# Conditioning vectors stationary, weights streamed in four column groups: the adaLN products of a two-layer flow block

## The reference, cut to what matters

```python
def ada_params(cond, w, b):            # w: (1024, 6144) per layer
    m = jax.nn.silu(cond) @ w + b
    return [t[:, None, :] for t in jnp.split(m, 6, axis=-1)]

sh1, sc1, g1, sh2, sc2, g2 = ada_params(c, ada_w[i], ada_b[i])
csh1, csc1, cg1, csh2, csc2, cg2 = ada_params(c_ctx[None, :], ada_w[i], ada_b[i])
a = modulate(rmsnorm(h), sh1, sc1)     # h * (1 + scale) + shift
h = h + g1 * rmsnorm(mixer(a))
h = h + g2 * rmsnorm(ffn(modulate(rmsnorm(h), sh2, sc2)))
```

## Time and profile before

| | |
|---|---|
| runs | 2705.26, 2714.47, 2714.45 us; median 2714.45 |
| profiled execution | span 2699.9 us from the first to the last instruction; the median lies 14.6 us above it |
| PE busy | 2432.5 us, 90% of the span |
| DVE, ACT busy | 1322.1 us (49%), 1144.3 us (42%) |
| chain that ended last | PE 79%, DVE 9%, ACT 6%, issue 4% |
| HBM read | 470 MB, 175 GB/s over the span |

### The profile page before, as it was taken

The page is one execution under the profiler, slowest core; times in us unless marked ns, Lnnn a source line. Parts: engine busy times, 40 slices in busy tenths (PEclk is TensorE's granted clock), DMA queues, the critical chain, the costliest instruction groups (busy, mean ns, idle before and its releaser), DMA issues.

```text
span 2699.9 us, 29721 instructions
## 1 busy us (share of the span) xinstructions
PE 2432.5 (90%) x10632; PEld 1840.9 (68%) x10633; DVE 1322.1 (49%) x1694; ACT 1144.3 (42%) x1436; POOL 36.1 (1%) x32
## 2 busy tenths in 40 slices
PE   4899977969999999688968999999999999999997
PEld 1455655538888888354657878787877777878785
DVE  1111045031111123315727878787964446878786
ACT  1201114141111112414435767676753335767675
POOL 0000013000000000000000000000000000000000
PEclk9998988878898889898979999999999999999999
DMA  6232300213333332210015979797964445979783
GB/s 225 94 125 94 125 0 1 82 43 121 120 132 124 125 125 94 90 63 1 12 54 207 359 281 363 269 366 272 362 229 156 164 163 189 359 280 357 295 344 138
DMA packets 68226, 472.56 MB, mean 175 GB/s; under 512 B 8119, under 2 KB 10328, under 8 KB 11544
## 3 DMA queue, kind: packets, MB, share of 16 engines
q1 hardware_dynamic: 64560, 463.50, 46.2%
q10 hardware_dynamic: 3560, 7.76, 0.8%
HBM read 470.18 MB, written 1.05 MB: 175 GB/s over the span
## 4 chain that ended last, share of the span: by engine, by line
PE 79%; DVE 9%; ACT 6%; issue 4%; ACTq 1%; DMA 1%; POOL 1%; DVEq 0%; POOLq 0%
PE bank L366 49%; PE bank L437 7%; PE bank L359 3%; PE bank L575 2%; PE bank L869 2%; DVE w_lo L1641 2%; PE bank L608 2%; ACT w_hi L1161 2%; PE bank L376 1%; PE bank L651 1%; PE bank L408 1%; PE bank L771 1%; PE bank L751 1%; PE bank L845 1%; DVE hT L1304 1%
## 5 line engine op out<-in xcount | busy, mean ns | idle before, releaser
L1641 DVE TENSOR_TENSOR w_lo<-ring,w_hi 128x1024 fp32r<-128x1024 f32 x672 | 797.4, 1222 | 208.1 <-ACT w_hi L1161 182.7
L1161 ACT ACTIVATE w_hi<-ring 128x1024 fp32r<-128x1024 f32 x672 | 697.7, 1059 | 266.0 <-PE bank L366 266.0
L366 PE MATMUL bank<-w_hi,x_hi 128*128 128x512 f32 x1008 | 409.6, 406 | 44.8 <-DVE x_lo L1682 24.3
L366 PE MATMUL bank<-w_hi,x_lo 128*128 128x512 f32 x1008 | 399.0, 396 | 0.0
L366 PE MATMUL bank<-w_lo,x_hi 128*128 128x512 f32 x1008 | 398.5, 395 | 0.0
L366 PEld LDWEIGHTS bank<-w_hi,x_hi 128*128 128x128 f32 x1008 | 193.3, 192 | 100.6 <-issue 43.3
L366 PEld LDWEIGHTS bank<-w_hi,x_lo 128*128 128x128 f32 x1008 | 192.8, 191 | 42.6
L366 PEld LDWEIGHTS bank<-w_lo,x_hi 128*128 128x128 f32 x1008 | 193.7, 192 | 38.4
L366 PE MATMUL bank<-w_hi,h_hi 128*128 128x512 f32 x504 | 196.9, 391 | 13.0 <-DVE h_lo L1655 13.0
L366 PE MATMUL bank<-w_hi,h_lo 128*128 128x512 f32 x504 | 196.7, 390 | 0.0
L366 PE MATMUL bank<-w_lo,h_hi 128*128 128x512 f32 x504 | 196.1, 389 | 0.0
(11 more groups left out here) (283 smaller groups left out, 2957.1 us busy)
## 6 DMA issues: line engine op xcount, KB each, us to landing
ring<-in_moe SPq DMA_DIRECT2D x336, 1024.0 KB, 5.5
ring<-in_pre SPq DMA_DIRECT2D x105, 1024.0 KB, 4.8
hT<-in_xT ACTq DMA_DIRECT2D x1, 2048.0 KB
out_T<-hT SPq DMA_DIRECT2D x2, 512.0 KB, 2.9
arena<-in_q_up ACTq DMA_DIRECT2D x1, 768.0 KB, 5.3
arena<-in_w_krv ACTq DMA_DIRECT2D x1, 640.0 KB, 3.8
mT<-in_decay ACTq DMA_DIRECT2D x1, 512.0 KB
arena<-in_dft ACTq DMA_DIRECT2D x1, 512.0 KB
```

The source lines that it names most:

```text
L366: m = pe.matmul(out, x[a], w[b], start=(first and n == 0), stop=(last and n == 2))
L1161: act.activation(w_hi[:, h % 4, :], ring[:, s % SLOTS, (h % 2) * UNIT:(h % 2 + 1) * UNIT], ACT.Copy).then_inc(sem("w_high"), 1)
L1641: dve.tensor_tensor(w_lo[:, h % 4, :], ring[:, (N_PRE + n) % SLOTS, (h % 2) * UNIT:(h % 2 + 1) * UNIT], w_hi[:, h % 4, :].bitcast(F32), AL ...
```

## The change

1. All 48 ada slots are now done with the conditioning vectors stationary. `cond32` holds the two vectors in a 32-column block with zeros behind them. A slot holds four of the eight 128-feature blocks of the contraction for 512 outputs. The four matmuls of a slot (`ada_half`) write partitions 0 to 31, 32 to 63, 64 to 95 and 96 to 127 of one bank, 512 columns each; the second slot of a group adds onto it. So a group is two slots and 512 outputs, and there are 12 groups per layer (`ADA_G`).
2. ACT copies the 128x512 bank to SBUF, and four matmuls with 2 columns (`ada_columns`) sum the four partial results and turn them, with `pick`, a 128x2 sum of four unit columns, as moving operand.
3. The groups lie elsewhere: 4 ahead of the input projection (as many slots as before), 8 in the SSD loop, one per two rows, 1 behind the first norm sum after the output projection, 11 in the dense SwiGLU, one per two steps. Nothing is interleaved with the input and output projections any more.
4. The gate/up split parts have two buffers (`gw_hi`, `gw_lo`; the second lies in `aT`), and ACT and DVE prepare step q+1 while PE does step q.

```diff
@@ PE @@
-            def ada_slot(s, dst, j, rounds=0):
-                slot_wait(s, rounds)
-                for h in range(2):
-                    for k in range(KD):
-                        m = pe.matmul(dst[:, 2 * (j + h):2 * (j + h) + 2], slot_tile(s, h, k), cond[:, k, :],
-                                      start=(k == 0), stop=(k == KD - 1))
+            def ada_half(g, half, dst):
+                for j in range(4):
+                    m = pe.matmul(dst[32 * j:32 * j + 32, :], cond32[:, 4 * half + j, :],
+                                  ring[:, (ada_slot(g) + half) % SLOTS, j * 512:(j + 1) * 512],
+                                  start=(half == 0), stop=(half == 1))
                 m.then_inc(sem("slot_used"), 1)
+            def ada_columns(g, i=None):
+                for t in range(4):
+                    at = 8 * (g % ADA_G) + 2 * t
+                    cols = slice(at, at + 2) if i is None else bass.ds(i * 24 + at, 2)
+                    m = pe.matmul(bank[6][:, cols], ada_rows(g)[:, t * P:(t + 1) * P], pick, start=True, stop=True)
+                m.then_inc(sem("ada_turned"), 1)
...
@@ input projection, output projection @@
-                ada_slot(n + 1, bank[6], 2 * s)
...
-                ada_slot(n + 1, bank[6], 2 * (N_EVIN + s))
             norm_sum(POST0, lambda k: aT[:, k, :])
+            ada_group(ADA_G, ada_bank(ADA_G))
...
@@ SSD loop @@
                     rows(r + 3)
+                ada_group(G_EVIN + r // 2, bank[2 + r // 2 % 2])
+                if r:
+                    ada_turn(G_EVIN + r // 2 - 1)
...
@@ dense SwiGLU @@
+            def gate_up_pair(m, i=None):
+                e = 0 if i is None else i
+                pe.wait_ge(sem("hff_done"), e * 6 + (2 * m + 1))
+                gate_up(0, e * 12 + 4 * m)
+                pe.wait_ge(sem("ada_rows"), e * 3 + (ADA_G + m + 1))
+                ada_columns(G_FFN + m - 1, i)
+                pe.wait_ge(sem("hff_done"), e * 6 + (2 * m + 2))
+                gate_up(1, e * 12 + (4 * m + 2))
+                g = G_FFN + m
+                for half in range(2):
...
+                    ada_half(g, half, ada_bank(g))
...
@@ ACT, SSD loop and dense SwiGLU @@
+                if r >= 2 and r % 2 == 0:
+                    ada_copy(G_EVIN + r // 2 - 1, bank[2 + (r // 2 - 1) % 2])
...
+                for q in range(2, 8):
+                    if q % 2 == 0:
+                        ffn_rows(G_FFN + q // 2 - 1, i * 12, i * 3)
+                    ffn_silu(q, i * 12, i * 6)
+                    ffn_high(q + 2, i * 12, i * 32)
```

More of the change, by code:

```diff
@@ L389, in _ @@
                 m.then_inc(sem("filt_mm"), 1)
[L392 to L413, removed]
+            pe.wait_ge(sem("cond_ready"), 2)
+            for g in range(G_EVIN):
+                ada_group(g, bank[g % 2])
+                if g:
+                    ada_turn(g - 1)
+            ada_turn(G_EVIN - 1)
             norm_sum(PRE0, lambda k: aT[:, k, :])
@@ L591, in gate_up @@
                     for k in range(KD):
-                        m = split_products(bank[2 * half + h][:, :], [w[:, h, k * P:(k + 1) * P] for w in (fw_hi, fw_lo)],
+                        m = split_products(bank[2 * half + h][:, :], [w[:, h, k * P:(k + 1) * P] for w in (gw_hi[half], gw_lo[half])],
                                            [x[:, k, :] for x in (fx_hi, fx_lo)], k == 0, k == KD - 1)
                 m.then_inc(sem("slot_used"), 1)
+            def gate_up_pair(m, i=None):
[7 more added lines that the diff above has]
+                g = G_FFN + m
+                for half in range(2):
+                    s = ada_slot(g) + half
+                    pe.wait_ge(sem(f"slot{s % SLOTS}_in"), e * 32 + 16 * (s // SLOTS + 1))
+                    ada_half(g, half, ada_bank(g))
@@ L597, in _ @@
             GR = NFF // 6
             with pe.Fori(0, GR) as i:
[L599 to L617, removed]
+                for m in range(3):
+                    gate_up_pair(m, i)
+            for m in range(3 * GR, NFF // 2):
+                gate_up_pair(m)
+            ada_turn(2 * ADA_G - 1)
@@ L958, in _, with ada_copy @@
             squares(PRE0, lambda k: hT[:, k, :], lambda k: aT[:, k, :])
[L959 to L963, removed]
+            def ada_copy(g, src):
+                act.wait_ge(sem("slot_used"), ada_slot(g) + 2)
+                if g >= 2:
+                    act.wait_ge(sem("ada_turned"), g - 1)
+                act.activation(ada_rows(g), src[:, :], ACT.Copy).then_inc(sem("ada_rows"), 1)
+            for g in range(G_EVIN):
+                ada_copy(g, bank[g % 2])
             for i in range(5):
@@ L1061, in ffn_tile, with ffn_rows @@
                 act.activation(sg[:, q % 2, :], bank[2 * (q % 2)][:, :], ACT.Silu).then_inc(sem("sg_ready"), 1)
-            with act.Fori(0, NFF // 6) as i:
[L1064 to L1067, removed]
+            def ffn_rows(g, used, turned):
+                act.wait_ge(sem("slot_used"), used + (ada_slot(g) + 2))
+                act.wait_ge(sem("ada_turned"), turned + (g - 1))
+                act.activation(ada_rows(g), ada_bank(g)[:, :], ACT.Copy).then_inc(sem("ada_rows"), 1)
@@ L1068, in _ @@
+            for q in range(NFF // 6 * 6 + 2, NFF):
+                if q % 2 == 0:
+                    ffn_rows(G_FFN + q // 2 - 1, 0, 0)
+                ffn_silu(q, 0, 0)
+            ffn_rows(2 * ADA_G - 1, 0, 0)
             for f in range(NFF):
@@ L1878, in layout @@
     pair = lambda x, s: [x[2 * s], x[2 * s + 1]]
-    for s in range(N_ADA_A):
-        slots.append(pair(ada[0], s))
-    for s in range(N_EVIN):
-        slots += [pair(evin, s), pair(ada[0], N_ADA_A + s)]
-    for s in range(N_EVOUT):
-        slots += [pair(evout, s), pair(ada[0], N_ADA_A + N_EVIN + s)]
-    for j in range(NFF):
-        slots += [[gate[j], up[j]], pair(ada[1], j)]
-    for s in range(N_ADA_C):
-        slots.append(pair(ada[1], NFF + s))
+    ada_pair = lambda g: [(ada[g, h, :, 0], ada[g, h, :, 1]) for h in range(2)]
+    for g in range(G_EVIN):
+        slots += ada_pair(g)
+    slots += [pair(evin, s) for s in range(N_EVIN)]
+    for g in range(G_EVIN, ADA_G):
+        slots += ada_pair(g)
+    slots += [pair(evout, s) for s in range(N_EVOUT)]
+    slots += ada_pair(ADA_G)
+    for m in range(NFF // 2):
+        slots += [[gate[2 * m], up[2 * m]], [gate[2 * m + 1], up[2 * m + 1]]] + ada_pair(G_FFN + m)
     slots += [pair(down, s) for s in range(N_DOWN)]
```

134 lines of the change are left out of this document (91 added, 43 removed).

## The result

The changed kernel takes 2495.03 us, the median of four runs (2494.12 to 2498.01), beside 2709.86 us for the kernel before (2703.33 to 2714.47, four runs, three of them those ahead of the forecast). The ratio is 0.9212, with a 95% interval of 0.9193 to 0.9231. The forecast was 2540 with a range of 2515 to 2595: the sign and the mechanism came out, the size did not.

What follows compares the result with a forecast made beforehand. PE was taken to bound the stages with ada work, through stationary weight loads and a lowered clock. Stage terms summed to -174 us: span 2699.9 to 2526, plus 14.6 gives 2540 us, range 2515 to 2595.

Steps and rivals of the forecast that it cites:

- The group, the clock, the order: Ada work: 2.0 us a group, 0.87 a turn, `gate_up` at 11.27; full overlap and full clock had chance 0.66.
- partial overlap: Ada groups: calls start strictly in order, a group takes 2 us more; +46, 2586 us; chance 0.12.
- no overlap: Ada groups: column groups do not run side by side; +5.2 us a group, 120 in all, 2660; chance 0.07.
- a falling clock: `gate_up` stays at 12.8: +34 us in SwiGLU, perhaps +10 and +8 in the projections; 2575 to 2592; chance 0.10.
- the slower case: Ada groups: one MATMUL at a time at 1.2 GHz, 13.8 us a group; 2840 us in all; chance 0.02.
- First block, both projections, the stretch before the down product: Four stages: first ada block -17.4 us, input projection -56.7, output projection -24.9, 964.1 to 982.4 -12.0.
- The time, 14.6 above it as the median is: Whole kernel: measured time lies 14.6 us above the span, so a span of 2526 becomes 2540 us.
- The stages behind are untouched: Down product to router, and experts: no change, 0 us.
- Dense SwiGLU, -78: Dense SwiGLU: 11 pairs of steps at 25.4 us, with cold start and loop overhead 282 against 360.1 us: -78.
- The cold start: Start of the dense SwiGLU: 1.7 us added.
- SSD loop, +14: SSD loop: 8 groups and turns, 23 us of PE work, make PE the bound; 61 to 64 us, +14.
- 558 to 604, +1: Stage between output projection and dense SwiGLU: one group and one ACT copy, +1 us (0 to 3).

Runs made afterwards that it cites:

- the two experiments on the form: Changed kernel with all four calls of a slot in one column group: 2611.52 us; changed kernel with weights stationary, two-column calls: 2888.50 us.
- the four padded runs: 16 or 48 tiny activations on ACT ahead of everything: kernel before 2684.64 and 2685.65 us, changed kernel 2498.75 and 2537.37 us.

## Why the forecast was right in kind and too small

*The group, the clock, the order: right.* The forecast named the mechanism, and what failed are terms of the sum. The clock of the dense SwiGLU is 0.99, the input projection runs 14.0 us a slot, and the two experiments on the form bear out overlap (2611.5 against 2612) and clock. The rivals of partial overlap, no overlap, a falling clock and the slower case are out by the group's 1.85 us and by the clock of 0.99.

*First block, both projections, the stretch before the down product: right to about 1 us each.* Together -113.1 against -111.0.

*"The time, 14.6 above it as the median is": wrong.* In every run that gives both, the time is 1.7 to 2.2 us above the span (2494.12 and 2492.3 in the profiled run of the changed kernel). The 14.6 us lay between one fast execution of the kernel before and the median of its others, which scatter by 18 us, and I carried them over to a kernel whose runs scatter by 4. (The kernel before scatters with its clock: 2699.92 us at a granted clock of 0.929 over the whole run, 2713.47 at 0.923.) With 1.8 in its place the same sum gives 2528. This is 12.8 of the 45 us, and it needed no experiment, only the thought that a constant above a span is not a scatter.

*"The stages behind are untouched": wrong in effect.* Their instructions are untouched, their place in ACT's code is not. The sum had 0 for them, and it was -13.7 us, shown by the four padded runs.

*Dense SwiGLU, -78: 6.4 too little.* One error of counting: of its 11 groups the last stands behind 780.5, and I had put it into both stages (2.0 us). The group is 1.85 and not 2.0, the turn 0.79 and not 0.87 (2.4 us over the ten and eleven of them). Most of the rest is that the two `gate_up`s of a pair took 11.01 + 11.40 and not 2 x 11.27 (1.4 us over eleven pairs), and that the 1 us for the loop's overhead did not appear. The cold start was real and larger than allowed: the first `gate_up` takes 13.41 us, 2.4 above the next, where I had 1.7. (The forecast also read DVE and ACT as busy for at most a sixth of these stages; here DVE's 65.1 of 360.1 us is 18%, which changed nothing.)

*SSD loop, +14: 5.4 too much.* The loop took +11.4 (I had added 2 to 3 us for a first group at the cold clock, and it took 1.85 us like the others), and the stretch behind it -2.9, of which 1.9 are POOL's shorter idle stretch (2.77 to 0.92 us), which the forecast did not look at.

*558 to 604, +1: came out -3.7.* I charged a group and overlooked that the norm sum ahead of it now finds PE at the full clock (1.00 over the norm sum in place of 0.75), as the output projection runs at 0.96 in place of 0.83. The chain, before and after:

```profile
558.44 9.33 PE bank L376 x16
```

```profile
462.86 6.88 PE bank L428 x16
```

That is 2.4 of the 4.7 us; the rest I did not trace. The reasoning that I had used for `gate_up` applied here too.

Of the 33 us that stay once the offset is taken out, the experts are 13.7, the dense SwiGLU 6.4, the SSD loop 5.4, the stage ahead of it 3.2 (within the scatter of that stage) and the one ahead of the dense SwiGLU 4.7; the four stages called right give 2.1 more, and down product to router takes 1.6 back. What took the time out of the range are the first two errors, the constant of 14.6 us and the 0 for the experts: together 26.5 us. Without them the miss would be 18.5 us, and the range reached 25 below the forecast. What failed in the forecast as a whole is that nearly every small term was rounded to the cautious side, and that the one stage with no edit in it was given no range at all.

## What to carry to other kernels

When a weight matrix meets two vectors, hold the vectors and stream the weights, and spread the contraction over the four column groups: count both the instruction time and the clock of what comes behind. Before an edit is called neutral for a later stage, look at the instruction packets and at engine stops marked "issue" at that stage's loop edges; if they are there, try a few idle instructions ahead: 17 instructions more removed 14 us here, and 48 more on top brought 42. And take the offset between span and time from one and the same run.

## What the runs showed of the hardware

- The clock column reads 1.00 over the first stage of every kernel here, also where the rates are those of 1.2 GHz: 64 two-column MATMULs take 13.65 us in the first block of the variant with weights stationary, 0.213 each, against 3.47 for 32 (0.108) at full clock. Before the first change of the clock in a trace the rate has to be read from the instructions:

```profile
47.30:60.50 13.20, 13.20 (x63) 13.20 (x63) 2.64 (x4) 0.00 (x0) 0.00 (x0) 1.00 0.25 81
```

- Two-column MATMULs, back to back and with PE at 100% busy, fall from 2.4 to 1.2 GHz within a group of 64, and a run of 128 that starts at the lower clock stays there to its end (27.40 us).
- Four column groups of fp32 calls, two MATMULs to a call, overlap by a factor of 3.8 (6.99 to 1.85 us).
- Loading ACT's code again at the change of experts made an expert 2.5 to 4.9 us longer in the kernel before and 4.8 to 9.2 in the changed kernel with 48 more instructions ahead, and whether it happened went with the code's place.
